# Second MLA pair's projections at steps 65 to 69, values of three pairs in one pass, late units in another order

## The reference

```
xn  = rms_norm(x, attn_norm)
o_a = nsa_attention(...)                     # 8 heads, 3 branches
q   = rms_norm(cq,  q_norm)  @ w_uq          # MLA: 8 heads, 96 columns each
kv  = rms_norm(ckv, kv_norm) @ w_ukv         # 8 heads: 64 key and 64 value columns each
o_b = softmax(q @ k.T / sqrt(96) + causal) @ v
merged = sigmoid(gate_a) * (o_a @ nsa_w_o) + sigmoid(gate_b) * (o_b @ mla_w_o)
x = x + merged @ w_out
x = x + square(relu(rms_norm(x) @ w_up)) @ w_down
```

## Time and profile before

| | us |
|---|---|
| median of 3 runs | 1520.73 |
| lowest and highest run | 1520.36, 1522.28 |
| the profiled execution's own time | 1520.22 |
| its span in the trace | 1518.4 |
| PE busy | 1496.2 (99% of the span) |
| DVE, ACT, POOL busy | 892.4, 718.1, 438.4 |

### The profile page before, as it was taken

The page is one execution under the profiler, slowest core; times in us unless marked ns, Lnnn a source line. Parts: engine busy times, 40 slices in busy tenths (PEclk is TensorE's granted clock), DMA queues, the critical chain, the costliest instruction groups (busy, mean ns, idle before and its releaser), DMA issues.

```text
span 1518.4 us, 21125 instructions
## 1 busy us (share of the span) xinstructions
PE 1496.2 (99%) x7332; PEld 1252.0 (82%) x7332; DVE 892.4 (59%) x1539; ACT 718.1 (47%) x1308; POOL 438.4 (29%) x459
## 2 busy tenths in 40 slices
PE   8999999999999999999999999999999999999998
PEld 6888888887888888888888888888888888888887
DVE  6875766767553544535557776667575535354453
ACT  6864777873431222222366557877544222122222
POOL 1302667773020101101021046777711101010111
PEclk9999999999999999999999999999999999999999
DMA  5343222125232332333223421212432332333223
GB/s 211 100 151 135 71 80 64 56 99 173 91 98 97 97 97 97 97 97 97 97 84 125 173 84 65 76 63 63 132 118 91 98 97 97 97 97 97 97 97 111
DMA packets 43362, 154.29 MB, mean 102 GB/s; under 512 B 5440, under 2 KB 5440, under 8 KB 43280
## 3 DMA queue, kind: packets, MB, share of 16 engines
q1 hardware_dynamic: 37296, 133.77, 27.2%
q0 software_dynamic: 5696, 18.94, 3.4%
q10 hardware_dynamic: 288, 0.52, 0.1%
HBM read 142.73 MB, written 10.49 MB: 101 GB/s over the span
## 4 chain that ended last, share of the span: by engine, by line
PE 86%; DVE 4%; ACT 4%; issue 3%; DMA 1%; POOL 1%; POOLq 0%; DVEq 0%; SPq 0%; ACTq 0%
PE G L1481 14%; PE G L1482 13%; PE G L1483 13%; PE O L1482 9%; PE O L1481 9%; PE O L1483 9%; PE O L1769 3%; PE T L1745 3%; PE S L1720 2%; PE T L1481 2%; PE T L1483 2%; PE T L1482 2%; ACT F L668 1%; PE O L1556 1%; DVE F L1422 1%
## 5 line engine op out<-in xcount | busy, mean ns | idle before, releaser
L616 ACT ACTIVATE wsplit<-stage 128x1024 fp32r<-128x1024 f32 x227 | 240.2, 1058 | 598.8 <-PE G L1483 270.7
L977 DVE TENSOR_TENSOR wsplit<-stage,wsplit 128x1024 fp32r<-128x1024 f32 x180 | 262.4, 1458 | 72.9 <-ACT wsplit L616 72.6
L602 POOL TENSOR_TENSOR F<-Y 128x512 f32<-128x512 f32 x64 | 68.5, 1070 | 637.4 <-DVE Y L1439 637.4
L1481 PE MATMUL G<-xg,wsplit 128*128 128x512 f32 x560 | 223.5, 399 | 7.4 <-DVE wsplit L1003 7.0
L1482 PE MATMUL G<-xg,wsplit 128*128 128x512 f32 x560 | 219.1, 391 | 0.0
L1483 PE MATMUL G<-xg,wsplit 128*128 128x512 f32 x560 | 219.0, 391 | 0.0
L1214 DVE CUSTOM_DVE_ANT_0 F<-S,F 128x512 f32<-128x512 f32 x192 | 93.6, 487 | 99.2 <-PE S L1720 68.2
L500 POOL TENSOR_TENSOR wsplit<-stage,wsplit 128x1024 fp32r<-128x1024 f32 x46 | 111.3, 2420 | 126.4 <-ACT wsplit L616 126.3
L787 ACT ACTIVATE F<-F,nmx 128x512 f32<-128x512 f32 x192 | 107.7, 561 | 66.3 <-DVE nmx L1214 64.8
L1481 PEld LDWEIGHTS G<-xg,wsplit 128*128 128x128 f32 x560 | 105.6, 189 | 28.9 <-DVE wsplit L1003 7.0
L1481 PE MATMUL G<-area,wsplit 128*128 128x512 f32 x320 | 124.7, 390 | 0.3
(11 more groups left out here) (292 smaller groups left out, 3049.4 us busy)
## 6 DMA issues: line engine op xcount, KB each, us to landing
stage<-units SPq DMA_DIRECT2D x229, 512.0 KB, 3.5
stage_n<-units_n SPq DMA_DIRECT2D x20, 512.0 KB, 3.9
gates<-Y POOLq DMA_DIRECT2D x32, 256.0 KB, 3.0
E<-gates POOLq DMA_DIRECT2D x24, 256.0 KB, 3.5
F<-gates POOLq DMA_DIRECT2D x8, 256.0 KB, 3.7
x<-x_in SPq DMA_DIRECT2D x3, 512.0 KB, 6.4
rope<-tables POOLq DMA_DIRECT2D x1, 768.0 KB, 6.2
out<-F SPq DMA_DIRECT2D x3, 256.0 KB, 2.1
```

Source lines behind the costliest of these rows:

```text
L602: pool.tensor_tensor(F[:, m % 2, :], Y[:, m % 2, :], Y[:, m % 2, :], ALU.mult)\
L616: act.activation(wslot(u)[:, 0, :], staged(u), ACT.Copy).then_inc(s_whin if u in SN else s_whi, 1)
L977: dve.tensor_tensor(wslot(u)[:, 1, :], staged(u), wslot(u)[:, 0, :], ALU.subtract)\
L1481: pe.matmul(dst, a(0), b(0), start=first, stop=False)
```

## The change

- The value columns of pairs 1, 2 and 3 stand together in the unit of pair 2 (384 columns). They are computed there in four pieces, V3 to V0, one for each tile of 128 tokens: three matmuls of 384 columns each. The pieces write tiles ("MV", 1, tt). ACT and DVE each empty such a tile with two instructions (256 and 128 columns wide) instead of one of 512. Pair 0 stays as it was. `MV[3]` lies in the second half of `pcT`.
- The order of the pieces is changed, and with it the banks, the steps of the units' splitting, and the order in which tiles are emptied. `KEY_STEP` of pair 1's first key part is 65 instead of 67.

The diff, cut to its core:

```diff
+MLA_KINDS = [("Q0", "Q1", "K", "V"), ("Q0", "K", "Q1"), ("V3", "V2", "Q0", "V1", "K", "V0", "Q1"), ("Q0", "K", "Q1")]
-for item, steps in ((("MLA", 1), (65, 66, 67, 71)), (("MLA", 2), (73, 74, 75, 78)), (("WA", 0), (76, 77, 79, 80)),
-                    (("MLA", 3), (81, 82, 83, 86)), (("WA", 1), (84, 85, 87, 88)), (("WA", 2), (90, 91, 93, 94)),
+for item, steps in ((("MLA", 1), (65, 67, 69)), (("MLA", 2), (71, 72, 73, 74, 75, 76, 77)), (("WA", 0), (78, 79, 80, 81)),
+                    (("MLA", 3), (82, 83, 84)), (("WA", 1), (85, 86, 87, 88)), (("WA", 2), (90, 91, 93, 94)),
+SPLIT_STEP[UNIT["MLA", 2]] = 68
-            (1, 0): FIRST_STEP["MLA", 1] + 2, (1, 1): FIRST_STEP["MLA", 1] + 5}
+            (1, 0): FIRST_STEP["MLA", 1], (1, 1): FIRST_STEP["MLA", 1] + 5}
...
@@ ACT, mla_v(p, tt), for the joint tiles
+                        act.wait_ge(s_mvals, l * QT + (QT - tt))
+                        src = g_tile(("MV", 1, tt))[:, 0:384].rearrange("p (a e n) -> p a e n", e=2, n=HD)
+                        act.activation(MV12[:, tt, :, :, 0:HD], src[:, 0:2], ACT.Copy)
+                        act.activation(MV[3][:, tt, :, 0:HD], src[:, 2], ACT.Copy).then_inc(s_mhi, 1)
...
@@ DVE, mla_v(p, tt)
+                        dve.tensor_tensor(MV12[:, tt, :, :, HD:P], src[:, 0:2], MV12[:, tt, :, :, 0:HD], ALU.subtract)
+                        dve.tensor_tensor(MV[3][:, tt, :, HD:P], src[:, 2], MV[3][:, tt, :, 0:HD], ALU.subtract)\
+                            .then_inc(s_gfree, 1)
...
@@ PE, mla(p, piece)
+                    elif kind[0] == "V" and kind != "V":
+                        tt = int(kind[1])
+                        three(dst[:, 0:384], lambda c: cn[:, c, 2, tt * P:(tt + 1) * P], lambda c: wslot(u)[:, c, 640:1024],
+                              True, True).then_inc(s_mvals, 1)
...
@@ PE, values(j)
-                    v = VN[:, kt, br, t // 2, :] if nsa else MV[t % 2][:, kt, e, :]
+                    v = VN[:, kt, br, t // 2, :] if nsa else MV[t][:, kt, e, :]
```

More of the change, by code:

```diff
@@ L120, in tile_of @@
     if name == "MLA":
-        return [("MQ", i, 0), ("MQ", i, 1), ("MK", i, 0), ("MV", i, 0)][piece]
+        kind = MLA_KINDS[i][piece]
+        if kind in ("V0", "V1", "V2", "V3"):
+            return ("MV", 1, int(kind[1]))
+        return {"Q0": ("MQ", i, 0), "Q1": ("MQ", i, 1), "K": ("MK", i, 0), "V": ("MV", 0, 0)}[kind]
     if name == "WA":
@@ L169 @@
 QK_AFTER = [NSA_NJ // 2, NSA_NJ, NSA_NJ + 8, NSA_NJ + 16]
-V_AFTER = [8, NSA_NJ // QT, NSA_NJ // QT + 2, NSA_NJ // QT + 4]
+V_AFTER = [8, NSA_NJ // QT]
+READY = [(p, kind) for p in range(PAIRS) for kind in MLA_KINDS[p][:-1] if kind[0] != "V"]
+MREADY = {t: n + 1 for n, t in enumerate(READY)}
+NMREADY = len(READY)
 MHI, MLO = {}, {}
@@ L818, in mla_k, with mla_v @@
                     ins.then_inc(s_mhi, 1)
-                def mla_v(p):
+                def mla_v(p, tt):
                     act.wait_ge(s_pv, l * NHP + V_AFTER[p])
[L822 to L825, removed]
+                    if p == 0:
+                        act.wait_ge(s_wused, l * NU + (UNIT["MLA", 0] + 1 + WUSED0))
+                        src = g_tile(("MV", 0, 0))[:, :].rearrange("p (a n) -> p a n", n=HD)
+                        act.activation(MV[0][:, :, :, 0:HD].rearrange("p t e n -> p (t e) n"), src, ACT.Copy).then_inc(s_mhi, 1)
+                    else:
+                        act.wait_ge(s_mvals, l * QT + (QT - tt))
+                        src = g_tile(("MV", 1, tt))[:, 0:384].rearrange("p (a e n) -> p a e n", e=2, n=HD)
+                        act.activation(MV12[:, tt, :, :, 0:HD], src[:, 0:2], ACT.Copy)
+                        act.activation(MV[3][:, tt, :, 0:HD], src[:, 2], ACT.Copy).then_inc(s_mhi, 1)
                 act.wait_ge(s_init, 2)
@@ L1239, in mla_rotate @@
                         dve.wait_ge(s_mlo, l * NMLO + (MLO["MQ", p - 1, e] + 1))
-                    dve.wait_ge(s_mready, l * 12 + (3 * p + e + 1))
+                    if p > 0 and e == 1:
+                        dve.wait_ge(s_wused, l * NU + (UNIT["MLA", p] + 1 + WUSED0))
+                    else:
+                        dve.wait_ge(s_mready, l * NMREADY + MREADY[p, ("Q0", "Q1")[e]])
                     dve.tensor_tensor(E[:, e, :], g_tile(("MQ", p, e))[:, :], tabM, ALU.mult).then_inc(s_gfree, 1)
@@ L1265, in mla_k, with mla_v @@
                     ins.then_inc(s_gfree, 1)
[L1267 to L1271, removed]
+                def mla_v(p, tt):
+                    dve.wait_ge(s_mhi, l * NMHI + (MHI["MV", p, tt] + 1))
+                    if p == 0:
+                        src = g_tile(("MV", 0, 0))[:, :].rearrange("p (a n) -> p a n", n=HD)
+                        both = MV[0][:, :, :, :].rearrange("p t e n -> p (t e) n")
+                        dve.tensor_tensor(both[:, :, HD:P], src, both[:, :, 0:HD], ALU.subtract).then_inc(s_gfree, 1)
+                    else:
+                        src = g_tile(("MV", 1, tt))[:, 0:384].rearrange("p (a e n) -> p a e n", e=2, n=HD)
+                        dve.tensor_tensor(MV12[:, tt, :, :, HD:P], src[:, 0:2], MV12[:, tt, :, :, 0:HD], ALU.subtract)
+                        dve.tensor_tensor(MV[3][:, tt, :, HD:P], src[:, 2], MV[3][:, tt, :, 0:HD], ALU.subtract)\
+                            .then_inc(s_gfree, 1)
                 def merged_lo(m):
@@ L1649, in mla @@
                     dst = g_tile(tile_of(("MLA", p), piece))
-                    if piece < 2:
+                    kind = MLA_KINDS[p][piece]
+                    if kind in ("Q0", "Q1"):
                         for k in range(2):
-                            ins = three(dst[:, :], wtile(u, 2 * k + piece), rows(cn, k), k == 0, k == 1)
-                        ins.then_inc(s_mready, 1)
-                    elif piece == 2:
+                            ins = three(dst[:, :], wtile(u, 2 * k + ("Q0", "Q1").index(kind)), rows(cn, k), k == 0, k == 1)
+                        ins.then_inc(s_mready if (p, kind) in MREADY else s_wused, 1)
+                    elif kind[0] == "V" and kind != "V":
+                        tt = int(kind[1])
+                        three(dst[:, 0:384], lambda c: cn[:, c, 2, tt * P:(tt + 1) * P], lambda c: wslot(u)[:, c, 640:1024],
+                              True, True).then_inc(s_mvals, 1)
+                    elif kind == "K":
                         three(dst[:, :], wtile(u, 4), rows(cn, 2), True, True).then_inc(s_mready, 1)
@@ L1758, in values @@
                         pe.wait_ge(s_ofree, l * NHEAD + (n - 1))
-                    if opens and not nsa and e == 0:
-                        emptied(("MV", t, 0))
+                    if opens and not nsa and e == 0 and t == 0:
+                        emptied(("MV", 0, 0))
+                    if not nsa and e == 0 and t == 1:
+                        emptied(("MV", 1, kt))
                     if nsa and br == 1 and kt == 0:
@@ L1964, in _units @@
             uq = _columns(w["mla_w_uq"][l], np.concatenate([192 * p + head, 192 * p + 96 + head]))
-            kv = [256 * p + 128 * e + o + r(64) for o in (0, 64) for e in range(2)]
+            kv = [256 * p + 128 * e + r(64) for e in range(2)]
+            for q in ([0], [], [1, 2, 3], [])[p]:
+                kv += [256 * q + 128 * e + 64 + r(64) for e in range(2)]
             put(UNIT["MLA", p], np.concatenate([uq, _columns(w["mla_w_ukv"][l], np.concatenate(kv))], axis=1))
```

12 lines of the change are left out of this document (8 added, 4 removed).

## The result

| | before | after |
|---|---|---|
| median, us | 1520.92 | 1524.63 |
| lowest and highest of 13 runs each | 1519.64, 1522.38 | 1523.24, 1527.95 |
| span of the profiled execution | 1518.4 | 1523.0 |

The ratio is 1.0025, with a 95% interval of 1.0018 to 1.0033: the kernel became slower by about 3.7 us. The forecast was 1524.4.

A forecast was written before the change was run, and what follows sets the result against it. PE, busy 99% of the span, was taken as the bound. About +1.9 us a layer, +3.8 in all, on 1520.2 gave 1524.0, and 0.5 for the median made it 1524.4; range 1516.5 to 1527.5.

The forecast's parts named there:

- Part 1: Value matmuls of each layer: twelve of 384 columns take 2.10 us instead of 4.02, saving PE 1.92 us.
- a saving of nothing: Rival, chance 0.02: the 384-column matmuls save nothing, so 1.92 us a layer are lost, 1528.2 us.
- Part 2: Old waits: step 81's 1.00 us goes, and of step 70's 1.69 us about 0.5 is left.
- (a): Step 71: PE waits 0.6 us for unit MLA2, split at 68, whose rest POOL makes.
- (b): Step 73: MQ(2,0) waits 2.3 us for V3's tile in bank 0 to be emptied by ACT and DVE.
- (c): Step 77: MQ(2,1) waits 2.4 us in bank 0 until MK(2)'s tile of step 75 is empty.
- (e): Step 85: A(2) waits 0.8 us behind the key tile MK(3) of step 83 (bounds 0.2 and 1.4).
- The balance of a layer: Per layer: waits of 6.7 us, less 2.69 old waits and 1.92 of work, +2.1; by the walk +1.9.
- Half the waits: Rival, chance 0.23: V3's and MK(2)'s tiles are empty 1.2 us sooner each; each layer gains 0.9, 1518.9 us.
- no bank waits: Rival, chance 0.14: neither wait at steps 73 and 77 is there; 3.5 us a layer come off, 1513.7 us.
- POOL behind: Rival, chance 0.08: POOL's rest of WA0 and queued scalings come late at steps 74 and 76; 2 us a layer more, 1528.
- the signs of being wrong: ACT reaching V3 before 279, MK(2) empty in under 5 us, or steps 65 to 88 waiting under 4.6 us a layer.

The follow-up runs named there:

- e5: e4 with each joint value piece made of nine 128-column matmuls instead of three of 384; 1517.61 us, ratio to before 0.9975.
- e4: The change with WA0's hi part at step 74 instead of 71 and the key piece last in pairs 2 and 3; 1516.27 us, ratio to before 0.9961.
- e3: The change with each joint value piece made of nine 128-column matmuls instead of three of 384; 1524.14 us, ratio to before 1.0014.
- e6: e4 with unit MLA2's hi part made at step 66 instead of 68; 1516.62 us, ratio to before 0.9971.
- e8: e4 with unit MLA2's hi part made at step 67 instead of 68; 1517.58 us, ratio to before 0.9976.
- e1: The change with unit WA0's hi part made by ACT at the end of step 74 instead of 71; 1524.61 us, ratio to before 1.0019.
- e10: e6 with ACT's rotary key copy for the odd pairs' second head cut from 512 to 8 columns (wrong keys); 1515.64 us, ratio to before 0.9961.
- e2: The change with pair 2's key piece last: MQ(2,1) in step 75, MK(2) in step 77; 1520.07 us, ratio to before 0.9991.
- e7: The change with seven unused 512-column matmuls ahead of each wait in steps 73 and 77, 28 in all; 1522.94 us, ratio to before 1.0010.
- e9: e4 with unit MLA2's pieces in the order Q0, V3, V2, Q1, V1, V0, K; 1517.36 us, ratio to before 0.9973.

## Why the prediction was right, step by step

- **Part 1, 2.10 for 4.02 us.** Right in its size: the matmuls stand 0.175 us apart, and a saving of nothing is not borne out (e5, by 128 columns, takes 1.3 us more than e4). As a saving it was too simple: while PE waits behind it, e3 shows a quarter of it, 0.49 us a layer. The sum held because it carried the waits as absolute release times.
- **Part 2, the old waits.** Step 81's went, as said. At step 70 0.5 was to be left; 0.06 is.
- **(a) step 71, 0.6 us.** Measured 0.72; POOL ends the unit's rest at 276.88, and PE starts 0.11 later; e6 and e8, which split the unit earlier, don't have this wait. POOL's timeline after the change:

```profile
274.50 2.38 POOL L513 TENSOR_TENSOR wsplit<-stage,wsplit 128x1024 fp32r<-128x1024 f32 x1
```

- **(b) step 73, 2.3 us.** Measured 1.96. The mechanism is shown by e1 (WA0's hi part away, the wait 0.95 us shorter) and, in e6's kernel, by e10. Less the 0.61 us of the start, ACT reached V3 at 280.4 (predicted 280.6) and MQ(2,0) started at 281.7 (282.0).
- **(c) step 77, 2.4 us.** Measured 2.22; e2 takes it away. MK(2)'s tile was empty 6.16 us after the start of step 75 (285.97 to 290.74 + 1.39 = 292.13), 6.25 was predicted (285.55 to 291.8). Of these two lines of the trace after the change the first is ACT's copy of V3's tile, for (b), the second DVE's rest of MK(2)'s:

```profile
281.04 0.38 ACT L842 ACTIVATE area<-G 128x256 fp32r<-128x256 f32 x1
```

```profile
290.74 1.39 DVE L1284 TENSOR_TENSOR area<-G,area 64x512 fp32r<-64x512 f32 x2 [0.80 <-ACT area L830]
```

- **(e) step 85, 0.8 us.** Measured 0.92.
- **The balance of a layer, +1.9 to +2.1.** The late starts in layer 0 are 0.06 + 0.72 + 1.96 + 2.22 + 0.92, and 0.2 at step 67 that was not foreseen: 6.1. Less 2.69 and 1.92 that is +1.5, and the trace shows +1.51. The sum was over by 0.4 to 0.6 us a layer: steps 70, 73 and 77 were put 0.44, 0.34 and 0.18 too high and 0.1 was left for step 75, where nothing is seen, against 0.12 too little at each of steps 71 and 85 and the 0.2 at step 67.
- **What the sum had not.** The lower clock behind the new waits: 1.43 us in layer 1 of the profiled execution, 1.7 us by e7 in the median. 2 x 1.5 + 1.7 would be 4.7, measured are 3.7 by the ratio. The median of before that is taken off holds lower clock as well: its longer runs have the lower mean granted clock, and whether its wait of 1.5 us in step 70 at times does the same was not tried. So that 3.8 came out so near to 3.7 is luck in part: the waits and the saved work alone give 3.0, and a term too large by 0.8 stood for one left out.
- **Small slips.** The text says that most of PE's named waits lie at the change. At the change are 4.7 us of 15.3; one wait of 7.0 us, for the first weights, stands at the kernel's start. No term hangs on it. And 1520.2 + 3.8 + 0.5 is 1524.5, not 1524.4.
- **The rivals.** Half the waits, no bank waits and POOL behind are out: the named waits of 0.55, 1.80, 2.06 and 0.76 us idle are there, and the only one that hangs on POOL is that of step 71, which was in the forecast. Of the signs of being wrong none came: ACT reached V3 at 280.4 and not before 279, MK(2) took 6.16 us and not under 5, and the waits sum to 6.1 us a layer and not to less than 4.6.

Still open: why a wait of 1.94 us is followed by the lower clock in layer 1 and one of 2.06 in layer 0 of the same execution is not; where before's longer runs lose their time; and what holds ACT and DVE in steps 66 to 70, where no single copy was found that moves V3 by itself.

## What to carry to other kernels

Before pieces are put in another order, write down for each output tile when its bank is wanted again, and lay beside it the copying engine's whole queue up to that tile. Here a key tile needs about 6 us from its step's start to be empty, and a piece two places behind it comes after 4; putting the slow tile last in both pairs, with one unit's split three steps later, turned 0.25% slower into 0.39% faster by the ratios of the runs, 0.26% by the spans. Work taken from an engine just ahead of a wait is worth nothing until the wait is gone (V3, V2 and V0 in e3), and worth something where no wait follows (V1 in e3, and e5). Where runs scatter by more than the effect, compare the same stretch in two traces, and look at the granted clock in it first.

## What the chip showed that was not expected

PE idle for about 2 us can be dearer than 2 us. Behind waits of 1.94 us (the change, layer 1) and 2.15 and 2.14 us (e1) the granted clock was 0.53 to 0.56 over the next 3.6 us and 512-column matmuls stood 0.42 to 0.43 us apart instead of 0.23; behind waits of 2.06 us (the change, layer 0) and 1.80 us (the change and e2) it stayed at 1.00. It also fell without such a wait: in the final norm of before, e6 and e9, behind one-column matmuls and transposes, it was 0.55 to 0.59 over some 3.7 us, which cost 0.4 to 0.6 us by the end of the span. The Trainium skill (TensorE: Matmul & The Clock Gate, Wait — 56ns, not 53.3ns?) gives N / 1.2 GHz for back-to-back matmuls on a cold array, 426.7 ns for 512 columns; this trace agrees with 0.42 to 0.43 us. Idle time filled with matmuls that nobody reads (e7) brought the median 1.7 us down and the spread of the runs from 4.7 to 1.0 us.
